# Head norms of an attention stage: one fp32 product with ones, or two one-pass products, and one step later

## The chip, the cores and the metric

The kernel runs on one core of one Trainium2 chip. The metric is the time of one execution on the device in microseconds (us); the median of the runs counts. The engines are named as in the profile: PE (TensorE), ACT (ScalarE), DVE (VectorE), POOL (GpSimd), and SP, which only issues DMAs.

## The reference, cut to what matters

Two layers of a decoder trunk over 512 tokens. Four mixers share one input projection; one of them is a differential attention with 4 heads of 128 value channels. Each head's output is normalised over its own 128 channels:

```python
    a = p[:, :, 0] - lam * p[:, :, 1]
    return jnp.einsum('bhqk,bkhe->bqhe', a.astype(v.dtype), v)
...
o = rmsnorm(o, sub_g) * (1.0 - lambda_init)
```

Then come the output projection, the residual, and a gated feed-forward block.

## The kernel before

Channels lie on the 128 partitions and tokens on the free axis, so a head's output is one tile of 128x512. Every engine runs a list of its own, written out by hand, and semaphores tie the lists together; nothing is scheduled by a planner. The order in the list is the order of work.

Large matmuls are in three one-pass products: the weights as a rounded part `wh` (fp32r, written by ACT in `prep`) and a remainder `wl` (written by POOL in `low`), against a rounded part and a remainder of the activations. One such output tile is a *unit*.

The attention of a layer is a loop over 16 steps, n = 0 to 15, four steps for each head (n // 4 is the head, n % 4 the block of 128 queries). In step n:

- PE does `scores(n + 2)`, `turn(n)` (transposes of the probabilities), at n = 1, 5, 7, 9, 13 and 15 (`BESIDE`) a unit of the output projection, and `attend(n - 1)`. At n = 15 the unit stands ahead of `turn`.
- DVE does `combine(n + 1)` (two softmaxes into one, which `turn(n + 1)` waits for) and `maxima(n + 2)` (which `exps(n + 2)` on ACT waits for). At n % 4 == 0 `head_out` copies the finished head from bank 5 to `ssum`; at n % 4 == 3 `head_emit` scales it.
- ACT does `exps(n + 1)`, the copy of the transposed probabilities (line 1355), and some `prep`s. `scores(n + 2)` takes the banks that `exps(n)` has read.
- POOL does a `low` whenever its weights are there.

The norm of head h is spread over this loop: at n % 4 == 1 ACT squares `ssum` into `pad` (`head_square`, line 1331); at n % 4 == 2 PE, last in its step, multiplies the squares with a matrix of ones in fp32 (`head_sum`, line 963), and ACT takes the logarithm of the mean (`head_log`, line 1336); at n % 4 == 3 ACT makes the reciprocal root of it (`head_rms`, line 1340). For heads 0 to 2 that is n = 5, 6, 7, then 9, 10, 11, then 13, 14, 15; head 3 comes after the loop.

Two other places matter. The norms of q and k in the projection already use a rounded part and a remainder: ACT writes `sq_high` and the square, POOL the difference (line 549), and PE two products with `block_r` (lines 891 and 892). And `block_r`, the fp32r copy of a constant, is made by DVE in layer 0 at s = 8 of the projection, between two copies into `cbf` (lines 2009 and 1653) and ahead of `lambdas` (lines 1656 and 1657). The next step of DVE's list is the scaling of `u` (line 1467) and `m2_turned(2)` (lines 1735 to 1738), which frees bank 4 for `m2_decays(0)` on PE (line 852). POOL meanwhile computes a table (lines 460 to 462) and the remainders of the weights (line 428).

Of the kernel before, what the change touches and what calls it, by code (L numbers as in the profile page):

```python
# [7 lines left out]
F32 = mybir.dt.float32  # L8
F32R = mybir.dt.float32r
BF16 = mybir.dt.bfloat16  # L10
ALU = mybir.AluOpType
ACT = mybir.ActivationFunctionType
# [3 lines left out]
D, T, P = 1024, 512, 128  # L16
KD = D // P
NQ = T // P
HEADS, QK = 4, 64
# [18 lines left out]
BESIDE = [1, 5, 7, 9, 13, STEPS - 1]  # L38
GATES = 3
V_BANK = [0, 1, 6, 7]  # L40
HEAD_BANK = [0, 0, 2, 6]
WHOLE_MEAN = 5
EPS = 1e-6
NIN = 28
FINE, COARSE = 32, 16
# [32 lines left out]
def build(nc, A):  # L78
    with ExitStack() as ctx:
        arena_end = [0]  # L80

        def sb(name, shape, dt=F32, at=None):

            size = int(np.prod(shape[1:])) * (2 if dt == BF16 else 4)
            size = -(-size // 32) * 32
            off = arena_end[0] if at is None else at
            if at is None:
                arena_end[0] += size
            offsets[name] = off
            return nc.alloc_sbuf_tensor_at(name, list(shape), dt, offset=base + off)  # L90

        def sem(name):
            return ctx.enter_context(nc.semaphore(name))
# [57 lines left out]
        for l in range(L):  # L151
# [28 lines left out]
        block_r = sb("block_r", [P, P], F32R)  # L180
        raw2 = sb("raw2", [P, FHALF * P], at=offsets["wglu"])
        raws = [raw[:, 0, :], raw[:, 1, :], raw2[:, :]]
        t_at = [offsets["qk"] + i * 3 * HT * 4 for i in range(2 * KW - 1)] + [offsets["G"] + 4 * T * 4]
        t_his = [sb(f"t_high{k}", [P, 3 * HT], F32R, at=t_at[KW + k]) for k in range(KW)]
        t_los = [sb(f"t_low{k}", [P, 3 * HT], F32R, at=t_at[k]) for k in range(KW)]
# [64 lines left out]
        exp_go, exp_done, probs_ready, probs_turned = [  # L250
            sem(n) for n in ("exp_go", "exp_done", "probs_ready", "probs_turned")]
        token_ready = sem("token_ready")
        head_copied, osq_ready, head_ln, onorm_done = [
            sem(n) for n in ("head_copied", "osq_ready", "head_ln", "onorm_done")]
        g_ready, g_silu, h_ready, h_high, hid_ready = [
            sem(n) for n in ("g_ready", "g_silu", "h_ready", "h_high", "hid_ready")]

# [154 lines left out]
        def _(pool):  # L412
# [112 lines left out]
            for l in range(L):  # L525
                low()
                for s in range(NIN - 1):
                    low()
                    if s == 1:
                        power_terms(l, 0)  # L530
                        nc.gpsimd.memset(kernels[:, :, :, :], 0.0)
                    if 2 <= s <= 4:
                        for n in ((1, 2), (3,), (4, 5))[s - 2]:
                            power_terms(l, n)
                    if s == 5:
                        pool.wait_ge(late_loaded, 32)
                        output_matrix(l)
                    if 6 <= s <= 8:
                        state_terms(l, s - 6)
                    if 9 <= s <= 10:  # L540
                        table(l, 0, s - 9)
                    if 11 <= s <= 12:
                        for n in ((3, 4), (5,))[s - 11]:
                            state_terms(l, n)
                    if 13 <= s <= 14:
                        table(l, 1, s - 13)
                    if 17 <= s <= 24 and s - 17 != WHOLE_MEAN:
                        pool.wait_ge(sqk_ready, 8 * l + s - 16)
                        tt(sq_low[:, :], G[:, 2, :], sq_high[:, :].bitcast(F32), ALU.subtract).then_inc(sqk_low, 1)
                    if s in (15, 21):  # L550
                        s5_imaginary(l, (s - 15) // 6)
                for _ in range(16):
                    low()
                for half in range(2):
                    for _ in range(2 * FHALF):
                        low()
                    if (l, half) in PAIRED:
                        pair_lows(UNIT_AT.index((l, NIN + 16 + 2 * FHALF)) if half == 0 else len(UNITS))
                    else:
                        for _ in range(8):  # L560
                            low()
# [3 lines left out]
        def _(pe):  # L565
# [358 lines left out]
            def scores(n):  # L924
                h, q = n // NQ, n % NQ
                banks = (2, 3, 6, 7)[2 * (n % 2):2 * (n % 2) + 2]
                rows = [slice(QK * c, QK * c + QK) for c in range(2)]
                qs = [qk[r, 2 * h, q * P:(q + 1) * P] for r in rows]
                last = slice(q * P, (q + 1) * P)
                for b in banks:  # L930
                    claim(b, exp_done)
                if q:
                    for c, b in enumerate(banks):
                        mm(bank[b][:, 0:q * P], qs[c], qk[rows[c], 2 * h + 1, 0:q * P], start=True, stop=True)
                for c, b in enumerate(banks):
                    mm(bank[b][:, last], qs[c], qk[rows[c], 2 * h + 1, last], start=True, stop=False)
                for b in banks:
                    mm(bank[b][:, last], cbf[:, 0, :], cbf[:, 1, :], start=False, stop=True).then_inc(dve_bank[b], 1)
# [18 lines left out]
                if q == NQ - 1:  # L957
                    w.then_inc(dve_bank[5], 1)

            def head_sum(b):  # L960
                pe.wait_ge(osq_ready, nth(osq_ready))
                claim(b, head_ln)
                mm(bank[b][:, :], ones, pad[:, 0, 4:4 + T], start=True, stop=True).then_inc(act_bank[b], 1)

            early_hi, early_lo = mh[:, MIXB:MIXED, :], ml[:, MIXB:MIXED, :]
            for l in range(L):
# [73 lines left out]
                for n in range(STEPS):  # L1040
                    if n + 2 < STEPS:
                        scores(n + 2)
                    if n == BESIDE[-1]:
                        unit(1, KEARLY, early_hi, early_lo, resid)
                    turn(n)
                    if n == GATES:
                        s5_glu()
                    if n == BESIDE[0]:
                        pe.wait_ge(mixed_ready, nth(mixed_ready, KEARLY))
                    if n in BESIDE[:-1]:  # L1050
                        unit(BESIDE.index(n) % 2, KEARLY, early_hi, early_lo, resid)
                    if n == 1:
                        pe.wait_ge(v_ready, HEADS * (l + 1))
                    if n:
                        attend(l, n - 1)
                    if n > NQ and n % NQ == 2:
                        head_sum(HEAD_BANK[n // NQ - 1])
                attend(l, STEPS - 1)
                unit(0, KEARLY, early_hi, early_lo, resid)
                head_sum(HEAD_BANK[HEADS - 1])  # L1060
# [15 lines left out]
        def _(act):  # L1076
# [127 lines left out]
            for l in range(L):  # L1204
# [121 lines left out]
                        fn(G[:, 2 * s + c, 0:w], bank[(2, 3, 6, 7)[2 * s + c]][:, 0:w], ACT.Exp,  # L1326
                           bias=soft[:, s, c:c + 1], accum_out=soft[:, s, 2 + c:3 + c]).then_inc(exp_done, 1)

                def head_square():
                    act.wait_ge(head_copied, nth(head_copied))  # L1330
                    fn(pad[:, 0, 4:4 + T], ssum[:, :], ACT.Square).then_inc(osq_ready, 1)


                def head_log(b):
                    act.wait_ge(act_bank[b], nth(act_bank[b]))
                    fn(rbc[:, :], bank[b][:, :], ACT.Ln, scale=1.0 / P, bias=eps).then_inc(head_ln, 1)

                def head_rms(h):
                    act.wait_ge(head_ln, l * HEADS + h + 1)
                    fn(rbc[:, :], rbc[:, :], ACT.Exp, scale=-0.5).then_inc(onorm_done, 1)  # L1340
# [7 lines left out]
                for n in range(STEPS):  # L1348
                    if n + 1 < STEPS:
                        exps(n + 1)  # L1350
                    if n > NQ and n % NQ == 3:
                        head_rms(n // NQ - 1)
                    act.wait_ge(act_bank[4], nth(act_bank[4]))
                    w = (n % NQ + 1) * P
                    fn(G[:, 4 + n % 2, 0:w], bank[4][:, 0:w], ACT.Copy).then_inc(probs_turned, 1)
                    if n == GATES:
                        for i, gate in enumerate((sA, sB)):
                            act.wait_ge(act_bank[i], nth(act_bank[i]))
                            fn(gate[:, :], bank[i][:, :], ACT.Sigmoid, bias=par_of(l, "bglu", i)).then_inc(glu_full, 1)
                        ln_exp_tables()  # L1360
                    if n == GATES + 1:
                        for i, gated in enumerate((sC, sD)):
                            emit(MIXC + i, gated[:, :])
                    if n > NQ and n % NQ == 1:
                        head_square()
                    if n - 1 in BESIDE:
                        prep()
                    if n > NQ and n % NQ == 2:
                        head_log(HEAD_BANK[n // NQ - 1])
                    if n > NQ and n % NQ == 0:  # L1370
                        emit(MIXA + n // NQ - 2, ssum[:, :])
                emit(MIXA + HEADS - 2, ssum[:, :])
# [60 lines left out]
        def _(dve):  # L1433
# [543 lines left out]
            for l in range(L):  # L1977
# [4 lines left out]
                for s in range(2, NIN):  # L1982
# [24 lines left out]
                    if l == 0 and s == 8:  # L2007
                        dve.wait_ge(cst_loaded, 16)
                        copy(cbf[:, 0, :], ident)
                        copy(block_r[:, :], block1).then_inc(block_ready, 1)  # L2010
                        lambdas()
                    if s == 9:
# [241 lines left out]
```

## Time and profile before

| what | us |
|---|---|
| median of 3 runs | 1303.96 (1303.4 to 1304.52) |
| profiled execution | 1304.08 |
| its span, first to last instruction | 1302.3 |
| PE busy | 1280.8 (98%) |
| DVE busy | 995.7 (76%) |
| POOL busy | 637.1 (49%) |
| ACT busy | 534.4 (41%) |

The profile is of one execution. What lies around the span is 1.8 us. The granted clock of PE is 1.00 of full speed over the whole span. Matmuls are pipelined, so a row of PE is longer than the time by which it holds up the next one; the distance of two starts tells that.

### The profile page before, as it was taken

Reading aid. Unit: us, or ns where it says so; the run is one execution under the profiler, and the core shown is the slowest. Engines: PE = TensorE matmul, PEld = TensorE weight load, DVE = VectorE, ACT = ScalarE, POOL = GpSimd, SP = SyncE. Lnnn points to the kernel's source line nnn. Section 1 sums busy time; section 2 is a strip of 40 time slices with the busy share of each in tenths; the row PEclk is TensorE's granted clock in tenths of the full one; section 3 lists DMA queues with packets and bytes.
Section 4 is the critical chain, followed back from the end, with each engine's and each line's share of the span. In section 5 each row is a group of like instructions: output and inputs, shape, how many; then the busy total and the mean of one; then the engine's idle time right before and its main releaser. Section 6 shows DMA issues by size and latency. Waiting matters only on the chain.

```text
span 1302.3 us, 17612 instructions
## 1 busy us (share of the span) xinstructions
PE 1280.8 (98%) x6758; PEld 1071.3 (82%) x6758; DVE 995.7 (76%) x1376; ACT 534.4 (41%) x836; POOL 637.1 (49%) x314
## 2 busy tenths in 40 slices
PE   7999999999999999999999999999999999999999
PEld 4878887788888998888878888867888889988898
DVE  7889894846899868886237798767478997689987
ACT  6332556644233332233334335476442333323332
POOL 2986662144445344444458775612354443444532
PEclk9999999999999999999999999999999999999999
DMA  6232231023333223233223213201333323232323
GB/s 212 79 109 67 81 95 44 25 86 109 99 95 132 90 88 97 95 100 112 84 97 97 82 53 112 79 26 50 98 105 97 97 99 114 95 93 89 125 92 104
DMA packets 40947, 120.59 MB, mean 93 GB/s; under 512 B 6432, under 2 KB 10656, under 8 KB 40864
## 3 DMA queue, kind: packets, MB, share of 16 engines
q1 hardware_dynamic: 40864, 119.46, 29.1%
q8 instruction: 54, 0.88, 0.3%
q14 instruction: 29, 0.24, 0.1%
HBM read 114.20 MB, written 2.10 MB: 89 GB/s over the span
## 4 chain that ended last, share of the span: by engine, by line
PE 75%; DVE 18%; ACT 2%; POOL 2%; issue 2%; DMA 1%; SPq 0%; DVEq 0%; POOLq 0%
PE bank L595 18%; PE bank L608 17%; PE bank L600 16%; PE bank L646 9%; PE bank L907 3%; DVE G L1479 3%; DVE bank L1851 2%; DVE G L1950 1%; DVE G L1478 1%; ACT G L1326 1%; PE bank L955 1%; DMA raw<-in_w_in 1%; PE bank L597 1%; POOL wl L428 1%; DVE G L1467 1%
## 5 line engine op out<-in xcount | busy, mean ns | idle before, releaser
L428 POOL TENSOR_TENSOR wl<-raw,wh 128x1024 fp32r<-128x1024 f32 (+3 forms) x184 | 442.2, 2405 | 520.7 <-ACT wh L1097 427.3
L595 PE MATMUL bank<-xl,wh 128*128 128x512 f32 x1088 | 281.7, 397 | 0.0
L608 PE MATMUL bank<-xh,wl 128*128 128x512 f32 x1088 | 272.4, 392 | 0.0
L600 PE MATMUL bank<-xh,wh 128*128 128x512 f32 x1056 | 261.0, 389 | 0.0
L1097 ACT ACTIVATE wh<-raw 128x1024 fp32r<-128x1024 f32 (+3 forms) x184 | 185.8, 1010 | 144.6 <-PE bank L600 90.9
L595 PEld LDWEIGHTS bank<-xl,wh 128*128 128x128 f32 x1088 | 202.8, 188 | 47.1 <-issue 5.4
L608 PEld LDWEIGHTS bank<-xh,wl 128*128 128x128 f32 x1088 | 203.2, 188 | 43.0 <-issue 1.4
L600 PEld LDWEIGHTS bank<-xh,wh 128*128 128x128 f32 x1056 | 198.2, 188 | 41.6
L445 POOL TENSOR_TENSOR wl<-raw,wh 128x768 fp32r<-128x768 f32 (+1 forms) x36 | 64.9, 1811 | 101.9 <-ACT wh L1101 70.0
L1398 ACT ACTIVATE G<-G 128x512 f32<-128x512 f32 x44 | 27.8, 633 | 181.3 <-DVE G L1479 181.3
L1101 ACT ACTIVATE wh<-raw 128x640 fp32r<-128x640 f32 (+2 forms) x72 | 60.5, 861 | 94.2 <-DVE raw L1917 37.1
L1496 DVE TENSOR_TENSOR x<-x,bank 128x512 f32<-128x512 f32 x40 | 27.4, 684 | 80.2 <-PE bank L608 80.0
L1467 DVE TENSOR_TENSOR G<-bank,rbc 128x512 f32<-128x512 f32 x68 | 46.4, 683 | 34.2 <-PE bank L608 34.2
L1467 DVE TENSOR_TENSOR pad<-bank,rbc 128x512 f32<-128x512 f32 x60 | 41.1, 686 | 38.2 <-PE bank L608 27.3
L595 PE MATMUL bank<-ml,wh 128*128 128x512 f32 x248 | 68.9, 401 | 0.0
L1479 DVE SCALAR_TENSOR_TENSOR G<-pad,par_all,G 128x512 f32<-128x512 f32 x48 | 66.5, 1385 | 1.7
L1474 DVE TENSOR_SCALAR G<-pad,par_all 128x512 f32<-128x512 f32 x48 | 65.5, 1364 | 1.6
L608 PE MATMUL bank<-mh,wl 128*128 128x512 f32 x248 | 63.2, 389 | 0.0
L1899 DVE TENSOR_TENSOR x<-x,bank 128x256 f32<-128x256 f32 (+1 forms) x72 | 41.7, 593 | 24.4 <-PE bank L663 17.0
L600 PE MATMUL bank<-mh,wh 128*128 128x512 f32 x225 | 57.1, 390 | 0.0
L1159 ACT ACTIVATE xh<-x,par_all 128x512 fp32r<-128x512 f32 x32 | 23.1, 721 | 80.0 <-DVE x L1496 77.6
L608 PEld LDWEIGHTS bank<-mh,wl 128*128 128x128 f32 x248 | 46.5, 188 | 9.7
(343 smaller groups left out, 2093.8 us busy)
## 6 DMA issues: line engine op xcount, KB each, us to landing
raw<-in_w_gu SPq DMA_DIRECT2D x88, 512.0 KB, 3.6
raw<-in_w_in SPq DMA_DIRECT2D x52, 512.0 KB, 3.7
raw<-in_w_dn SPq DMA_DIRECT2D x32, 704.0 KB, 4.2
raw<-in_w_ol SPq DMA_DIRECT2D x16, 384.0 KB, 3.0
raw<-in_w_oe SPq DMA_DIRECT2D x16, 256.0 KB, 2.6
x<-in_x SPq DMA_DIRECT2D x8, 256.0 KB, 6.4
raw<-in_w_first SPq DMA_DIRECT2D x4, 512.0 KB, 4.7
out_x<-x SPq DMA_DIRECT2D x8, 256.0 KB, 4.6
```

The lines of the kernel that those rows point to most:

```text
L428: tt(wl[:, p, 0:cols], raws[RAW[g][0]][:, 0:cols], wh[:, p, 0:cols].bitcast(F32), ALU.subtract).then_inc(wl_full, 1)
L445: tt(wl[:, p, cols], raws[PAIR_RAW[load][0]][:, cols], wh[:, p, cols].bitcast(F32), ALU.subtract).then_inc(pair_low, 1)
L595: mm(bank[b][:, :], wh[:, p, k * P:(k + 1) * P], lo[:, k, :], start=(k == 0), stop=False)
L600: w = mm(bank[b][:, :], wh[:, p, k * P:(k + 1) * P], hi[:, k, :], start=False, stop=False)
L608: w = mm(bank[b][:, :], wl[:, p, k * P:(k + 1) * P], hi[:, k, :], start=False, stop=(k == K - 1))
L646: i = mm(out, w[:, at[0], at[1] + k * P:at[1] + (k + 1) * P], b, start=start and k == 0, stop=stop and k == KW - 1, skip_group_check=True)
L1097: fn(wh[:, p, 0:cols], raws[r][:, 0:cols], ACT.Copy).then_inc(wh_full, 1)
L1101: fn(wh[:, p, to], raws[PAIR_RAW[2 * j + p][0]][:, of], ACT.Copy).then_inc(pair_high, 1)
L1467: tt(out, bank[b][:, :].rearrange(order, **sizes), rbc[:, :].rearrange(order, **sizes), MUL).then_inc(unit_out, 1)
L1474: after(ts(out, pad[:, p, 4:4 + T], weights[n - 1], None, MUL))
L1479: return stt(out, pad[:, p, 5 - n:5 - n + T], weights[0], out, MUL, ADD)
L1899: tt(out, out, b, ADD).then_inc(pair_read, 1)
```

## The change

For heads 0 to 2, `head_square` writes the square twice: rounded to fp32r into `xh[:, 0, :]`, and whole into `pad`. POOL writes the difference into `xl[:, 0, :]`, in its list ahead of the `low`s 3, 5 and 6 of the output projection. PE multiplies both parts with `ones_r`, an fp32r copy of the ones, in two one-pass products into one bank. `head_sum` moves from the end of step n % 4 == 2 to step n % 4 == 3, behind `scores(n + 2)` and ahead of the unit of n = 15 and of `turn(n)`. `head_log` moves from the end of ACT's step n % 4 == 2 into n % 4 == 3, behind `exps(n + 1)` and right ahead of `head_rms`. The banks are 1, 0, 0 instead of 0, 0, 2. Head 3 stays as it was. `ones_r` is made by DVE right ahead of `block_r`.

```diff
-HEAD_BANK = [0, 0, 2, 6]
+HEAD_BANK = [1, 0, 0, 6]
+HEAD_LOW = [3, 5, 6]
...
+        ones_r = sb("ones_r", [P, P], F32R)
...
-                for _ in range(16):
+                for n in range(16):
+                    if n in HEAD_LOW:
+                        pool.wait_ge(osq_ready, l * HEADS + HEAD_LOW.index(n) + 1)
+                        tt(xl[:, 0, :], pad[:, 0, 4:4 + T], xh[:, 0, :].bitcast(F32), ALU.subtract).then_inc(osq_low, 1)
                     low()
...
-            def head_sum(b):
+            def head_sum(b, parts=False):
+                if parts:
+                    nth(osq_ready)
+                    pe.wait_ge(osq_low, nth(osq_low))
+                    claim(b, head_ln)
+                    mm(bank[b][:, :], ones_r[:, :], xh[:, 0, :], start=True, stop=False)
+                    mm(bank[b][:, :], ones_r[:, :], xl[:, 0, :], start=False, stop=True).then_inc(act_bank[b], 1)
+                    return
...
                     if n + 2 < STEPS:
                         scores(n + 2)
+                    if n > NQ and n % NQ == 3:
+                        head_sum(HEAD_BANK[n // NQ - 1], True)
                     if n == BESIDE[-1]:
                         unit(1, KEARLY, early_hi, early_lo, resid)
                     turn(n)
...
-                    if n > NQ and n % NQ == 2:
-                        head_sum(HEAD_BANK[n // NQ - 1])
...
-                def head_square():
+                def head_square(parts=False):
                     act.wait_ge(head_copied, nth(head_copied))
+                    if parts:
+                        fn(xh[:, 0, :], ssum[:, :], ACT.Square)
                     fn(pad[:, 0, 4:4 + T], ssum[:, :], ACT.Square).then_inc(osq_ready, 1)
...
                     if n > NQ and n % NQ == 3:
+                        head_log(HEAD_BANK[n // NQ - 1])
                         head_rms(n // NQ - 1)
...
                     if n > NQ and n % NQ == 1:
-                        head_square()
+                        head_square(True)
                     if n - 1 in BESIDE:
                         prep()
-                    if n > NQ and n % NQ == 2:
-                        head_log(HEAD_BANK[n // NQ - 1])
...
                         copy(cbf[:, 0, :], ident)
+                        copy(ones_r[:, :], ones)
                         copy(block_r[:, :], block1).then_inc(block_ready, 1)
```

## Rows read from the trace of the kernel before

**Rows 1.** The page: the span, and the chain that ended last, shares by engine.
```profile
span 1302.3 us, 17612 instructions
...
PE 75%; DVE 18%; ACT 2%; POOL 2%; issue 2%; DMA 1%; SPq 0%; DVEq 0%; POOLq 0%
```

**Rows 2.** Waits, 76 to 90 us: us in total, times, longest.
```profile
PE bank L852 <- DVE xbt L1738: 1.1, 1, 1.1
```

**Rows 3.** The chain in order of time, layer 0: start us, us, what.
```profile
248.51 0.86 PE bank L963 x2
```

**Rows 4.** Timeline of PE, q/k norms: start us, us, engine, line.
```profile
146.10 0.39 PE L891 MATMUL bank<-sqk_high,block_r 128*128 128x512 f32 x1
146.33 0.39 PE L892 MATMUL bank<-sqk_low,block_r 128*128 128x512 f32 x1
```

**Rows 5.** Timeline of PE, attention of layer 0, [idle before <-releaser].
```profile
236.47 0.66 PE L944 MATMUL bank<-cst,G 128*128 128x128 f32 x4 [0.54 <-DVE G L1834]
...
249.30 0.49 PE L934 MATMUL bank<-qk 64*128 64x128 f32 x4
...
250.13 0.66 PE L944 MATMUL bank<-cst,G 128*128 128x128 f32 x4
...
253.62 0.92 PE L934 MATMUL bank<-qk 64*128 64x384 f32 x4
...
259.03 1.02 PE L963 MATMUL bank<-pad,cst 128*128 128x512 f32 x2
```

**Rows 6.** Timeline of ACT, attention of layer 0.
```profile
247.06 0.69 ACT L1326 ACTIVATE G<-bank,soft 128x512 f32<-128x512 f32 x1 [1.21 <-DVE soft L1825]
...
251.01 0.62 ACT L1340 ACTIVATE rbc<-rbc 128x512 f32<-128x512 f32 x1
251.53 0.59 ACT L1355 ACTIVATE G<-bank 128x512 f32<-128x512 f32 x1
252.46 0.47 ACT L1326 ACTIVATE G<-bank,soft 128x256 f32<-128x256 f32 x1 [0.33 <-DVE soft L1825]
...
256.93 0.63 ACT L1331 ACTIVATE pad<-ssum 128x512 f32<-128x512 f32 x1 [0.28 <-DVE ssum L1841]
...
261.00 0.69 ACT L1336 ACTIVATE rbc<-bank,eps 128x512 f32<-128x512 f32 x1
261.73 0.63 ACT L1340 ACTIVATE rbc<-rbc 128x512 f32<-128x512 f32 x1
```

**Rows 7.** Timeline of DVE, attention of layer 0.
```profile
243.12 1.35 DVE L1492 TENSOR_TENSOR ml<-ssum,mh 128x512 fp32r<-128x512 f32 x1 [0.50 <-ACT mh L1187]
...
248.74 0.55 DVE L1833 TENSOR_SCALAR G<-G,soft,mlam_all 128x512 f32<-128x512 f32 x1
249.33 0.75 DVE L1834 SCALAR_TENSOR_TENSOR G<-G,soft 128x512 f32<-128x512 f32 x1
```

**Rows 8.** Timeline of POOL: a remainder of the q/k norms, a weights' remainder.
```profile
149.23 1.30 POOL L549 TENSOR_TENSOR sqk_low<-G,sqk_high 128x512 fp32r<-128x512 f32 x1 [0.41 <-ACT G L1226]
...
242.64 1.27 POOL L428 TENSOR_TENSOR wl<-raw,wh 128x512 fp32r<-128x512 f32 x1 [5.09 <-ACT wh L1097]
```

**Rows 9.** Timeline of DVE, layer 0, s = 8 of the projection.
```profile
79.87 0.21 DVE L2010 CAST block_r<-cst 128x128 fp32r<-128x128 f32 x1
80.01 1.29 DVE L1653 CAST cbf<-pre 128x128 bf16<-128x128 f32 x1
81.22 0.28 DVE L1656 TENSOR_TENSOR lprod<-pre 128x128 f32<-128x128 f32 x1
...
81.85 2.05 DVE L1656 TENSOR_TENSOR lprod<-pre 128x128 f32<-128x128 f32 x1
```

**Rows 10.** Timeline of POOL in the same stretch.
```profile
79.94 1.27 POOL L462 TENSOR_TENSOR s5f<-s5f,s5h 128x512 f32<-128x512 f32 x1
81.29 2.46 POOL L428 TENSOR_TENSOR wl<-raw,wh 128x1024 fp32r<-128x1024 f32 x1
83.71 1.38 POOL L460 TENSOR_TENSOR s5g<-rot 128x512 f32<-128x512 f32 x1
```

More of the change, by code:

```diff
@@ L252, in build @@
         token_ready = sem("token_ready")
-        head_copied, osq_ready, head_ln, onorm_done = [
-            sem(n) for n in ("head_copied", "osq_ready", "head_ln", "onorm_done")]
+        head_copied, osq_ready, osq_low, head_ln, onorm_done = [
+            sem(n) for n in ("head_copied", "osq_ready", "osq_low", "head_ln", "onorm_done")]
         g_ready, g_silu, h_ready, h_high, hid_ready = [
```

## The prediction

> **What bounds the kernel now.** I read the page first: PE is busy for 98% of the span of 1302.3 us, and the chain that ended last runs over PE for 75% and over DVE for 18% [rows 1]. So a shorter product may pay, but only where PE doesn't wait for someone else straight after it. Then I read the waits and the timelines of all engines around each of the six products that change, and around the one new copy. The reader is to look there for who was late at the next hand-over, not at how busy an engine is.
>
> **The product itself.** The fp32 product with ones holds the chain for 0.86 us [rows 3]. Two one-pass products of the same shape already stand in the trace, 0.23 us apart [rows 4]; two of them are 0.46 us. Six products make 6 x 0.40 = 2.4 us, the most that the change can give. Where does it go?
>
> **Heads 0 and 1: the 0.40 us are lost in front of `turn`.** At step 7, `turn(7)` on PE waited 0.54 us for DVE's `combine(7)` [rows 5]. That combine hangs on `exps(7)` and DVE's own queue, neither of which needs `head_sum(0)`. Nothing that ends before that hand-over brings it forward. The moved product of 0.46 us fits into the wait of 0.54. Gain 0, loss 0. At step 11, `turn(11)` began at 250.13 [rows 5], 0.05 us after `combine(11)` ended (249.33 + 0.75 = 250.08 [rows 7]); I take 0.05 as the cost of a hand-over. Without `head_sum(1)` `scores(13)` (249.30 [rows 5]) may start up to 0.86 us sooner, but the new 0.46 us come behind it and `turn(11)` still waits for 250.08. Gain between 0 and 0.05; I take 0. On layer 1 the timeline repeats these starts 641.3 us later with the same gaps.
>
> **The second square on ACT** costs 0.52 us, the distance of two ACT instructions of 512 columns (251.01 to 251.53 [rows 6]). The next work, `exps` of the following step, had ACT idle for 1.21 us before it, waiting for DVE [rows 6]; that hides it. Were that idle time gone, it would cost 0.52 per head.
>
> **The logarithm moves behind `exps(n + 1)`.** There it takes 0.73 us (261.00 to 261.73 [rows 6]) ahead of the reciprocal root and of line 1355's copy. After head 1, the root was at 251.01 and the copy at 251.53 [rows 6]; they go to 251.74 and 252.26. The copy then ends at 252.85, and `exps(13)`, which started at 252.46 after 0.33 us of idle time, can't start before about 252.76 (the next instruction overlaps the tail by 0.10, as 0.62 against 0.52 shows). So `exps(13)` is 0.30 late, bounds 0 and 0.73. Who waits for it? `scores(15)` on PE, which started at 253.62 [rows 5], and `combine(13)` on DVE, from which DVE works without a gap to `combine(14)`, that is to `turn(14)`. I put the full 0.30 us on the path of each layer. After head 0 the same delay meets a unit on PE and a DVE that is busy with `residual`; I take 0 there. What is queued behind the logarithm on ACT is only this copy and the `exps`; the `prep` that stood ahead of it now runs no later.
>
> **Head 2: PE waits for POOL.** At n = 15 there are no `scores` left, so the product stands where it stood, directly behind `attend(13)`, at 259.03 [rows 5] + 0.30 = 259.33. The new remainder is not there yet: the square began at 256.93 [rows 6]; with 0.30 delay, a second square (0.52 later, 0.63 long, as the first) ends at 258.38; POOL starts at 258.43 and takes 1.30, like the same difference for q and k [rows 8], to 259.73; PE starts at 259.78 and is done at 260.24. Before it was 259.03 + 0.86 = 259.89. So head 2 saves nothing: +0.35 us against before, the 0.30 included. Two layers: **+0.70**. Bounds: 0 (ACT's overlap is larger) and 2 x 0.73 + 2 x 0.5 (nothing hidden) = 2.5.
>
> **POOL's list.** Each difference comes before a `low` whose weights ACT has not yet prepared (`low` 4 waited 5.09 us for them [rows 8]), so the queue behind the new wait is not held up, nor SP's loads, which wait for `low`. But POOL and DVE disturb each other: while POOL ran 242.64 to 243.91 [rows 8], DVE's subtraction of two SBUF operands took 1.35 us from 243.12 on [rows 7], some 0.67 more than the usual one. For head 1 the first square ended at 247.06 - 1.21 = 245.85 [rows 6], the second one ends at 246.37, POOL works from 246.42 to about 247.7, and DVE's next instruction on SBUF alone is at 248.74 [rows 7]. In between it works on PSUM. Cost 0, with 1.0 us in hand; bound 1.27 each.
>
> **The copy `ones_r` is the large term.** It looks like 0.14 us of DVE (79.87 to 80.01 [rows 9]), once. But `m2_decays(0)` on PE, line 852, waited 1.1 us for DVE at the end of just this sequence [rows 2], and no wait of PE stands between it and the attention, so what DVE loses here PE loses. And DVE doesn't lose 0.14. In the rows DVE's small instructions and POOL's take turns: `block_r` at 79.87 got in before POOL's 79.94; the next, at 80.01, took 1.29 us and ended at 81.30, when POOL's was over (79.94 + 1.27 = 81.21) [rows 9, 10]. The product at 81.22 got in before POOL's 81.29; the one at 81.85 took 2.05 us, to 83.90, over POOL's end at 83.75 [rows 9, 10]. With one more copy, `ones_r` takes the place of `block_r`, and `block_r` that of the cast at 80.01, to 81.30. The cast takes the place at 81.22, and the first product comes 0.14 later, at 81.36, behind POOL's 81.29. It ends at 83.90, where the second one used to end. The second follows 0.35 later (81.50 to 81.85 before), at 84.25, and POOL's next instruction holds until 83.71 + 1.38 = 85.09 [rows 10]; it ends at 85.24. DVE is 1.34 us late, and so is line 852. I take **+1.34**; bounds 0.14 (0 even, if the turn at 81.85 swallows it) and 2.64 (one more POOL instruction of 1.30 lost).
>
> The Trainium skill, page "SBUF — State Buffer", section "SBUF: two separate sides", says that the port pair which VectorE and GpSimd share is an exclusive lock held for a whole instruction, taken by whichever starts first, and that VectorE wants it with two SBUF inputs or in a two-port mode. The starts and ends above agree with it. By it the copy costs a turn; by the copy's own row, 0.14. It speaks against this change.
>
> **The sum:** 1304.08 (profiled execution; span plus 1.8 around it) + 0.70 + 1.34 = 1306.1. The median of the runs is 0.12 lower than that execution: **1306.0**, or 0.16% slower. A measurement of this kernel can tell about 0.2%, here 2.6 us: slower begins at 1306.6, faster ends at 1301.4.
>
> **Rivals.** *The copy is hidden.* If DVE keeps its turn at 81.36 (it lies only 0.07 behind POOL), the first product ends by 81.7, the second still ends at 83.90, and only the attention's 0.70 is left: 1304.7. For it: the margin is thin. Against: the cast at 80.01 lost with the same 0.07. *A second turn lost:* POOL's next instruction gets in before the product that waits at 85.09. +1.30, 1307.3, slower. Against it: at 83.71 the waiting DVE went first, and POOL's took 1.38. *Faster:* PE is the bound at each of the six places and no wait takes up the 0.40: 1304.0 - 2.4 = 1301.6, about at the edge of what can be told. Against it stand the 0.54 at step 7 and the 0.05 at step 11; it decides only if the `combine`s end 0.4 sooner. *POOL's difference blocks `combine`:* it would have to start after 248.74 - 1.27 = 247.47, which is 1.0 later than worked out; 1.27 for head 1 of each layer: 1308.5.
>
> **How the numbers follow.** Forecast 0.52, its own range 1305.2 to 1306.8; copy hidden 0.25; second turn lost 0.12; `combine` blocked 0.05; all six gained 0.03; and 0.03 for a gain of a part. From the forecast some 0.08 and from the two slow rivals 0.17 lie above 1306.6: slower 0.25. Faster 0.02. Same 0.73. The range for 8 in 10 takes in the hidden copy and most of the second turn: 1303.9 to 1307.4.
>
> **What would show it.** In the profile after: two products 0.23 apart between `scores(9)` and `turn(7)`, and `turn(7)` still waiting for DVE; ACT without idle time before `exps(13)`; PE waiting some 0.45 us for POOL's difference at n = 15; line 852 waiting 2.4 us instead of 1.1, and DVE's first line 1656 taking over 2 us. If line 852 still waits 1.1 to 1.3, the largest term is wrong. If `turn(7)` and `turn(11)` come sooner relative to the layer's first `scores`, the argument on heads 0 and 1 is wrong.

## The result and the profile after

The changed kernel takes 1307.58 us (median of 9 runs, 1306.32 to 1308.1), the kernel before 1303.84 us (9 runs): a ratio of 1.0028, 95% interval [1.002, 1.0036]. That is 3.7 us more; 2.0 us were forecast, with a range up to 1307.4, and a time more than 0.2% longer had been given a chance of 0.25. The profiled execution took 1307.58 us over a span of 1305.8 us, 3.5 us more than before.

The waits of PE in the changed kernel (line, whom it waited for: us in total, times, longest; line 719 of before is 724 now, 852 is 857, 934 is 939, 944 is 949, `head_sum` is 970 and 971):

```profile
PE bank L724 <- ACT wh L1109: 9.0, 1, 9.0
PE bank L939 <- ACT G L1338: 5.8, 10, 1.2
PE bank L857 <- DVE xbt L1751: 2.5, 1, 2.5
PE bank L970 <- DVE x L1509: 1.8, 2, 0.9
PE bank L651 <- DVE x L1912: 1.7, 3, 0.6
PE bank L949 <- DVE G L1847: 1.1, 2, 0.5
PE bank L949 <- ACT G L1370: 0.9, 2, 0.5
```

Line 857 waited 1.1 us before [rows 2] and waits 2.5 now, as forecast. But the products with ones wait for `DVE x`, that is for the residual, 0.9 us in each layer, and no step of the prediction knew of that. The two waits of 0.5 us for ACT's line 1370 are new too. That line 939 waits 5.8 us, where line 934 waited 4.1, is no loss: ahead of `scores(9)` stands a wait of 1.2 us in each layer, in the place that head 0's product has left.

To see where the time comes in, take the starts of the transposes: those of step 0 and step 15 of an attention enclose everything that the change moved. The kernel before, then the changed one, layer 0, from the timeline of PE:

```profile
211.83 0.33 PE L944 MATMUL bank<-cst,G 128*128 128x128 f32 x1
...
262.64 0.60 PE L944 MATMUL bank<-cst,G 128*128 128x128 f32 x4
```

```profile
213.08 0.33 PE L949 MATMUL bank<-cst,G 128*128 128x128 f32 x1
...
264.95 0.60 PE L949 MATMUL bank<-cst,G 128*128 128x128 f32 x4
```

Step 0 starts 1.25 us later, all of it from line 857. From there to step 15 it is 50.81 us before and 51.87 after: +1.06. Layer 1 gives 50.82 and 51.85, +1.03. The rest, between the layers and behind them, is 0.16. Together 3.50, the difference of the spans. So the term for the copy was right (1.34 forecast, 1.25 found), and the attention costs 1.05 per layer instead of 0.35.

**The copy.** DVE and POOL in s = 8 of the projection in the changed kernel, to set beside [rows 9, 10]:

```profile
79.87 0.21 DVE L2023 CAST ones_r<-cst 128x128 fp32r<-128x128 f32 x1
80.01 1.29 DVE L2024 CAST block_r<-cst 128x128 fp32r<-128x128 f32 x1
81.22 0.21 DVE L1666 CAST cbf<-pre 128x128 bf16<-128x128 f32 x1
81.36 2.48 DVE L1669 TENSOR_TENSOR lprod<-pre 128x128 f32<-128x128 f32 x1
...
84.20 0.96 DVE L1669 TENSOR_TENSOR lprod<-pre 128x128 f32<-128x128 f32 x1
```

```profile
79.95 1.28 POOL L464 TENSOR_TENSOR s5f<-s5f,s5h 128x512 f32<-128x512 f32 x1
81.30 2.39 POOL L430 TENSOR_TENSOR wl<-raw,wh 128x1024 fp32r<-128x1024 f32 x1
83.65 1.36 POOL L462 TENSOR_TENSOR s5g<-rot 128x512 f32<-128x512 f32 x1
```

`ones_r` has the place that `block_r` had, `block_r` the one of the long cast. The cast falls into the gap at 81.22, and the first product of the lambdas at 81.36 comes 0.06 behind POOL's 81.30: it takes 2.48 us. The second one then waits over POOL's 83.65 as well, until 85.16. An instruction of 0.14 us has cost 1.25.

**The attention.** PE in the changed kernel, layer 0, around the three products:

```profile
237.02 0.48 PE L970 MATMUL bank<-xh,ones_r 128*128 128x512 f32 x1
237.33 0.39 PE L971 MATMUL bank<-xl,ones_r 128*128 128x512 f32 x1
237.75 0.65 PE L949 MATMUL bank<-cst,G 128*128 128x128 f32 x4
...
251.43 0.66 PE L949 MATMUL bank<-cst,G 128*128 128x128 f32 x4
...
254.30 0.30 PE L949 MATMUL bank<-cst,G 128*128 128x128 f32 x1 [0.47 <-ACT G L1370]
...
259.81 0.52 PE L949 MATMUL bank<-cst,G 128*128 128x128 f32 x3
...
261.67 0.47 PE L970 MATMUL bank<-xh,ones_r 128*128 128x512 f32 x1 [0.89 <-DVE x L1509]
261.98 0.39 PE L971 MATMUL bank<-xl,ones_r 128*128 128x512 f32 x1
```

Heads 0 and 1 went as worked out: `turn(7)` and `turn(11)` start 1.28 and 1.30 us later than in [rows 5], which is the shift of step 0 with 0.03 and 0.05 more; the products fit into the waits and neither cost nor gave anything. Head 2 is where it went wrong. `turn(14)` starts at 259.81 (before 258.19), +1.62, so 0.37 came from the late `exps(13)` (0.30 forecast). Then the first product at 261.67 had 0.89 us of idle time before it, and what it waited for is bank 0. ACT, DVE and POOL at that point:

```profile
248.36 0.69 ACT L1338 ACTIVATE G<-bank,soft 128x512 f32<-128x512 f32 x1 [0.69 <-DVE soft L1838]
...
253.57 0.58 ACT L1370 ACTIVATE G<-bank 128x512 f32<-128x512 f32 x1
254.05 0.47 ACT L1338 ACTIVATE G<-bank,soft 128x256 f32<-128x256 f32 x1
...
259.06 0.62 ACT L1345 ACTIVATE pad<-ssum 128x512 f32<-128x512 f32 x1
```

```profile
260.84 0.68 DVE L1509 TENSOR_TENSOR x<-x,bank 128x512 f32<-128x512 f32 x1
```

```profile
259.75 1.27 POOL L557 TENSOR_TENSOR xl<-pad,xh 128x512 fp32r<-128x512 f32 x1 [7.24 <-ACT pad L1345]
```

POOL's difference was there at 259.75 + 1.27 = 261.02, but DVE's `residual`, which reads bank 0 after the unit of step 13, ran from 260.84 to 261.52. It stands in DVE's list behind `maxima(15)`, which DVE worked on until 260.93. The two products then held the unit behind them up by 0.53 us (261.67 to 262.20), not by 0.46. The copy at 253.57 is the one that `turn(12)` waited for (line 1370), and the `exps` at 248.36 still had 0.69 us of idle time ahead of it with a second square before it.

### The profile page after: what moved, and what is told of

Read it like the earlier page. It is cut to its first block, busy times and chain, and to the rows that moved or that the text cites. A ratio compares the mean times of both kernels' runs of the same rounds, so it can differ in the third digit from the quotient of the medians.

```text
span 1305.8 us, 17625 instructions
## 1 busy us (share of the span) xinstructions
PE 1279.3 (98%) x6758; PEld 1071.6 (82%) x6758; DVE 996.6 (76%) x1377; ACT 538.0 (41%) x842; POOL 648.4 (50%) x320
## 4 chain that ended last, share of the span: by engine, by line
PE 77%; DVE 15%; ACT 3%; POOL 2%; DMA 1%; issue 1%; SPq 0%; DVEq 0%; POOLq 0%
PE bank L600 19%; PE bank L613 19%; PE bank L605 18%; PE bank L651 10%; PE bank L912 3%; DVE bank L1864 2%; DVE G L1492 2%; ACT G L1338 1%; DMA raw<-in_w_in 1%; PE bank L602 1%; DVE soft L1838 1%; POOL wl L430 1%; DVE G L1491 1%; DVE G L1847 1%; DVE G L1846 1%
## 5 line engine op out<-in xcount | busy, mean ns | idle before, releaser
L1487 DVE TENSOR_SCALAR G<-pad,par_all 128x512 f32<-128x512 f32 x48 | 65.8, 1370 | 1.6
```

Of the source, the lines that this page charges most:

```text
L1487: after(ts(out, pad[:, p, 4:4 + T], weights[n - 1], None, MUL))
```

## The experiments

The measure for most of them is the time from the transposes of step 0 to those of step 15 in a layer: 50.81 us before (50.82 in layer 1), 51.87 and 51.85 in the changed kernel. The profiled execution gives this to a few hundredths, while whole runs scatter by about 1 us: in the traces with the wait at line 852 or 857, PE comes to it between 83.4 and 86.1 us, of which the wait at the very start (8.2 to 9.8 us) is a part. So the division of the loss rests on the profiled executions and their waits. The kernel before was run 21 to 29 times beside each group of experiments, medians 1303.4 to 1303.8.

**e1: the copy elsewhere.**

```diff
-                        copy(ones_r[:, :], ones)
                         copy(block_r[:, :], block1).then_inc(block_ready, 1)
...
+                if l == 0:
+                    copy(ones_r[:, :], ones)
                 maxima(0)
```

> The changed kernel, with the copy into ones_r taken out of s = 8 of the projection and put right ahead of the attention of layer 0. Theory (the copy costs DVE a turn against POOL, and line 857 on PE waits for that): 1.2 to 1.3 us less than the changed kernel, about 1306.3, and line 857 waits 1.1 us again instead of 2.45. Rival (the copy costs only its own 0.14 us, the later wait has another cause): 1307.4, line 857 waits over 2 us.

Measured: 1305.89 us, ratio 1.0016 [1.0007, 1.0025], by the two ratios 1.6 us less than the changed kernel. Its waits:

```profile
PE bank L970 <- DVE x L1509: 1.8, 2, 0.9
...
PE bank L857 <- DVE xbt L1751: 1.1, 1, 1.1
```

Line 857 is back at 1.1 us, the attention is as in the changed kernel (51.85 and 51.86). The rival falls.

**e2: bank 2 for head 2.**

```diff
-HEAD_BANK = [1, 0, 0, 6]
+HEAD_BANK = [1, 0, 2, 6]
```

> The changed kernel, with head 2's product in bank 2, as before the change, instead of bank 0. Theory (at n = 15 PE waits for DVE's residual, which reads bank 0 until 0.6 us after POOL's remainder is there): the wait before the first product is 0.3 to 0.4 us instead of 0.89 and names POOL; 0.5 to 0.6 us less in each layer, about 1306.5. Rival (PE waits for POOL's remainder there, the bank is free in time): no change, 1307.6.

Measured: 1306.83 us, ratio 1.0023 [1.0013, 1.0032]; 51.29 us in both layers, 0.57 less than the changed kernel. The product now waits for POOL, in the timeline of PE and of POOL:

```profile
261.84 0.50 PE L970 MATMUL bank<-xh,ones_r 128*128 128x512 f32 x1 [0.30 <-POOL xl L557]
262.18 0.39 PE L971 MATMUL bank<-xl,ones_r 128*128 128x512 f32 x1
```

```profile
260.52 1.27 POOL L557 TENSOR_TENSOR xl<-pad,xh 128x512 fp32r<-128x512 f32 x1 [7.24 <-ACT pad L1345]
```

POOL ends at 261.79 and the product starts at 261.84. In the changed kernel the bank came 0.5 us after this. That is the step that was missing.

The same trace shows a second price of the copy, which the changed kernel's own trace doesn't have. PE behind the wait of line 857, in the changed kernel and in e2:

```profile
87.42 1.16 PE L857 MATMUL bank<-cst,s 128*128 128x128 f32 x8 [2.45 <-DVE xbt L1751]
88.42 1.06 PE L849 MATMUL bank<-xbc 128*128 128x128 f32 x8
```

```profile
86.61 1.20 PE L857 MATMUL bank<-cst,s 128*128 128x128 f32 x8 [2.31 <-DVE xbt L1751]
87.60 1.91 PE L849 MATMUL bank<-xbc 128*128 128x128 f32 x8
```

The same eight products of line 849 take 1.91 us instead of 1.06, and the eight of line 613 behind them 2.94 instead of 2.09. In e2 PE stood idle for 2.31 us, worked for about 1 us with the granted clock still at 1.00, and then the clock was 0.50 of full speed from 88 to 91 us (the lower of its two levels, 1.2 GHz) and 1.00 again from there on. In the changed kernel it was 1.00 throughout. From line 857 to the transposes of step 0 it is 127.26 us in e2 and 125.66 in the changed kernel: 1.6 us. e4's trace has the same (127.27, idle time 2.35 us). Runs whose mean clock is below 1.00, as e2's and e4's profiled ones are, number 16 of 34 in the four kernels that have the copy at s = 8 (1 of 9 of the changed one, 5 of 9 of e2, 6 of 11 of e3, 4 of 5 of e4), and 1 of 112 in the other experiments. Why some executions fall into this and others with as long a wait don't was not tried.

**e3: the copy alone, in the kernel before.**

```diff
                         copy(cbf[:, 0, :], ident)
+                        copy(ones_r[:, :], ones)
                         copy(block_r[:, :], block1).then_inc(block_ready, 1)
```

> The kernel before, with only the copy into ones_r added ahead of block_r; nothing reads it. Theory (a lost turn): 1.2 to 1.3 us more than before, about 1305.1, the first product of line 1656 takes over 2 us. Rival (0.14 us, or hidden): 1303.8 to 1304.0.

Measured: 1305.93 us, ratio 1.002 [1.0011, 1.0029]. The wait, at line 853 here:

```profile
PE bank L853 <- DVE xbt L1739: 2.4, 1, 2.4
```

2.4 us instead of 1.1, and the attention untouched (50.83, 50.84). A copy that nothing reads costs 1.3 us by the wait. The whole runs give 2.5 (1.4 to 3.8), more than that. In this trace, whose clock was 1.00, the other 1.05 us lie ahead of the wait, which is within the scatter given above. But 6 of its 11 runs have a clock below 1.00; at 1.6 us each (an estimate from e2's trace) that is 0.9 us of the mean. So a copy of 0.14 us costs 1.2 to 1.3 us in each of the four traces that have it, and in 16 of 34 runs probably another 1.6.

**e4: ACT's copy first.**

```diff
-                    if n > NQ and n % NQ == 3:
-                        head_log(HEAD_BANK[n // NQ - 1])
-                        head_rms(n // NQ - 1)
                     act.wait_ge(act_bank[4], nth(act_bank[4]))
...
                     fn(G[:, 4 + n % 2, 0:w], bank[4][:, 0:w], ACT.Copy).then_inc(probs_turned, 1)
+                    if n > NQ and n % NQ == 3:
+                        head_log(HEAD_BANK[n // NQ - 1])
+                        head_rms(n // NQ - 1)
```

> The changed kernel, with ACT's copy of the transposed probabilities ahead of the logarithm and the root in steps 7, 11 and 15. turn(12) then no longer waits 0.47 us for that copy. Theory (what reaches turn(14) is the late exps(13), by way of DVE, and that stays): no change, within 0.2 us of 1307.6. Rival (the wait of turn(12) reaches the end): 0.4 to 0.5 us less in each layer, about 1306.7.

Measured: 1310.65 us, ratio 1.0055 [1.0041, 1.0068]. Both were wrong about the time, and the theory was right about its own point. `turn(12)` doesn't wait any more, and yet from step 0 to step 14 it takes 46.69 us, as in the changed kernel (46.73). `scores(15)` waits 0.37 us for `exps(13)` instead. But:

```profile
PE bank L975 <- ACT pad L1345: 2.8, 2, 1.4
```

At n = 15 the order matters in the other direction. The logarithm of head 2 now stands behind a copy that has to wait for the late `turn(15)`; so `head_emit`, DVE's copy of head 3 and its square come later, and PE waits 1.4 us per layer for that square. The expectation had looked only at head 1. Part of this run's time is also the lower clock of e2, in four of its five runs.

**e5: the split without the move.** `ones_r` made as in e1, the two products at the old place, banks 0, 0, 2, the logarithm at its old place:

```diff
-                    if n > NQ and n % NQ == 3:
-                        head_sum(HEAD_BANK[n // NQ - 1], True)
...
                         attend(l, n - 1)
+                    if n > NQ and n % NQ == 2:
+                        head_sum(HEAD_BANK[n // NQ - 1], True)
```

> The two one-pass products in the old place (end of step n % 4 == 2), the old banks and the old place of the logarithm; ones_r made right ahead of the attention. Only the split is left of the change. Theory (the 0.40 us that a product saves are taken by the wait for DVE's combine at heads 0 and 1, and by the wait for POOL's remainder at head 2): from the first to the last transposes of a layer's attention 50.8 to 51.0 us, as before (50.81), and 0 to 0.2 us per layer more than the kernel before: the same time as before within 0.4 us. Rival (the saving reaches the end where nothing is moved): 0.4 per head, 49.6 us per layer, 2.4 us less than before.

Measured: 1303.99 us, ratio 1.0006 [0.9997, 1.0015]; 51.03 and 50.97 us. Three shorter products give nothing, even where nothing is moved; it is 0.2 us per layer more than before. PE waits for POOL at heads 0 and 2 (1.2 us in 4 waits), and the other places are covered by the waits for `combine`.

**e6: the move without the split.** The kernel before with one fp32 product ahead of `turn(n)`, banks 1, 0, 0, the logarithm ahead of the root:

```diff
+                    if n > NQ and n % NQ == 3:
+                        head_sum(HEAD_BANK[n // NQ - 1])
                     if n == BESIDE[-1]:
...
-                    if n > NQ and n % NQ == 2:
-                        head_sum(HEAD_BANK[n // NQ - 1])
...
+                        head_log(HEAD_BANK[n // NQ - 1])
                         head_rms(n // NQ - 1)
```

> The kernel before with only the move: one fp32 product a step later, banks 1, 0, 0, the logarithm ahead of the root; no second square, no remainder, no ones_r. Theory (the move is what costs, by the bank that waits for DVE's residual at head 2, and here also by the longer product between the scores and the transposes at heads 0 and 1): from the first to the last transposes 52.8 us against 51.87 of the changed kernel and 50.81 before; about 4 us more than before. Rival (the remainder and the second square are what costs): no more than the changed kernel's attention without them, 50.8 to 51.3 us per layer.

Measured: 1306.97 us, ratio 1.0027 [1.0017, 1.0038]; 52.40 us in both layers, less than the 52.8 expected, since the longer product costs only 0.20 us in front of `turn(7)` (3.85 us from step 6 instead of 3.65). The move alone loses 1.6 us per layer. The same wait for the residual is there without POOL's remainder and without a second square:

```profile
259.57 1.10 PE L963 MATMUL bank<-pad,cst 128*128 128x512 f32 x2 [0.89 <-DVE x L1495]
```

**e7: the constants of layer 0 later.** The kernel before with this block of DVE behind `m2_turned(3)`:

```diff
-                    if l == 0 and s == 8:
-                        dve.wait_ge(cst_loaded, 16)
-                        copy(cbf[:, 0, :], ident)
-                        copy(block_r[:, :], block1).then_inc(block_ready, 1)
-                        lambdas()
```

> The kernel before, with the small copies and the lambda products of DVE in s = 8 of layer 0 put behind m2_turned(3) of s = 9; nothing else. Theory (PE's line 852 waits 1.1 us only because these instructions lose two turns against POOL ahead of m2_turned(2)): that wait is gone, 1.0 to 1.1 us less than before. Rival (DVE's scaling of u or POOL is what it waits for in the end): the wait stays above 0.5 us and the time is that of before.

Measured: 1302.94 us, ratio 0.9997 [0.9988, 1.0006]. The wait at line 852 is gone, but 0.8 us of it are found a few instructions on, at the next product that needs DVE:

```profile
PE bank L834 <- DVE hst L1752: 0.8, 1, 0.8
```

So the theory was right about line 852 and wrong about the gain, and the rival had the time right: it can't be told from that of before.

**e8: a run that was not what its expectation says.**

> The changed kernel with both mends: ones_r copied right ahead of the attention, head 2's product in bank 2. Theory (a lost turn of 1.3 us once, and 0.57 us per layer for the bank, are independent): 51.29 us from the first to the last transposes of a layer, line 857 waits 1.1 us; 1.0 to 1.1 us more than the kernel before, 2.4 less than the changed one. Rival (they hide one another): more than 1.6 us above the kernel before.

The kernel that ran had e4's order on ACT besides the two mends. Measured: 1307.81 us, ratio 1.0031 [1.0019, 1.0042], with e4's wait of 2.8 us in all for the square of head 3. It is 3.5 us more than e14, which differs from it by e4's order alone. So this order costs as much without the other two losses; of the mends themselves the run tells nothing. e14 below is the kernel that was meant.

**e9: head 2 alone, the remainder inside the next unit.** The kernel before, the constants as in e7 (with `ones_r`). Head 2's rounded part is multiplied at the old place in bank 2; the remainder's product comes inside the unit of n = 15:

```diff
+                    if middle is not None and part == 0:
+                        middle()
                     if ready is None:
...
+            def head_rest(b):
+                pe.wait_ge(osq_low, nth(osq_low))
+                mm(bank[b][:, :], ones_r[:, :], xl[:, 0, :], start=False, stop=True).then_inc(act_bank[b], 1)
```

> The kernel before with the constants as in the run above (with ones_r), and two one-pass products for head 2 alone: the rounded part's product in the old place and bank, the remainder's product inside the unit that follows, after its first pass of four products. Heads 0, 1 and 3 as before. Theory (head 2 is the one of heads 0 to 2 whose product PE does not wait after, and POOL's remainder is 0.5 us late only for the first place): 0.40 us less per layer from the first to the last transposes (50.4 instead of 50.81), together 1.8 to 1.9 us less than before. Rival (something behind head 2 takes it up, the logarithm or the root for the last head): only the 1.1 us of the constants.

Measured: 1303.16 us, ratio 0.9996 [0.9987, 1.0005]; 50.42 and 50.43 us. So one product does give its 0.39 us, at the only one of the three places where PE does not wait afterwards. The 1.1 us of the constants did not come: the wait at DVE's `hst` was 1.5 us here. The whole run can't be told from the kernel before, where 1.8 to 1.9 us less were expected.

**e13: no wait for POOL at head 2.** As e14 below, but head 2's second product takes `xh` again; the remainder is left out of it. PE takes POOL's semaphore only behind the unit that follows.

```diff
+                        mm(bank[b][:, :], ones_r[:, :], xh[:, 0, :], start=True, stop=False)
+                        mm(bank[b][:, :], ones_r[:, :], xh[:, 0, :], start=False, stop=True).then_inc(act_bank[b], 1)
```

> As the run before, but head 2's second product takes the rounded part once more instead of the remainder, so it leaves the remainder out and does not wait for POOL; the work of each engine stays the same. Theory (what is left of head 2's loss is 0.3 us of waiting for POOL): 51.0 us from the first to the last transposes instead of 51.29; the remaining 0.2 above the 50.81 of before is exps(13) behind the logarithm, less what the shorter product gives. Rival (all that is left comes from the late exps): 51.29, unchanged.

Measured: 1303.79 us, ratio 1.0002 [0.9993, 1.0011]; 50.71 and 50.69 us. The gain over e2 is 0.58, twice what I expected. The row of the wait says 0.30. But rows of PE are longer than what they hold up: with the wait gone the first product starts 0.72 us behind `turn(14)` (259.44 against 258.72), before the row of `attend(13)` ends, and in e2 it started 1.27 us behind it. Here the idle time in a row was only about half of what the wait cost.

**e14: both mends.**

> The changed kernel with the two mends alone: ones_r copied right ahead of the attention, head 2's product in bank 2; ACT's order as in the changed kernel. Theory (the lost turn and the bank are independent): 51.29 us from the first to the last transposes of each layer, line 857 waits 1.1 us, 0.9 to 1.1 us more than the kernel before. Rival (they hide one another): over 51.6 us or over 2 us of wait at line 857.

Measured: 1304.33 us, ratio 1.0004 [0.9996, 1.0013]; 51.26 and 51.28 us, line 857 waits 1.2 us. In the trace the two losses are independent and add up. With them gone whole runs can't be told from the kernel before; by the trace 0.45 us per layer is still lost.

**e15: the logarithm of heads 0 and 1 short.** As e14; those two take it of one column of 512 and leave out the rest.

```diff
+                    if h < 2:
+                        fn(rbc[:, 0:1], bank[b][:, 0:1], ACT.Ln, scale=1.0 / P, bias=eps).then_inc(head_ln, 1)
+                        return
```

> As the run before, but the logarithm of heads 0 and 1 is taken of one column of 512 only, so it leaves out the rest. Theory (the moved logarithm makes exps(13) some 0.3 to 0.4 us late and that reaches the transposes of step 14): from the transposes of step 0 to those of step 14 46.4 us as before the change (46.36) instead of 46.7; the first to the last 50.9 to 51.0. Rival (the second square or the longer way over POOL makes it late): 46.7, unchanged.

Measured: 1304.16 us, ratio 1.0003 [0.9994, 1.0012]; 46.36 and 46.39 us from step 0 to step 14, before the change 46.36, with the whole logarithm 46.72. So up to step 14 the logarithm ahead of `exps(13)` costs 0.36 us (0.32 in layer 1), and the second square none of it. Up to step 15 the run takes 50.97 and 51.02 us, 0.29 and 0.26 less than e14: a little of it is taken up at head 2.

**e11: two copies to where DVE is idle.** The kernel before, with two of the copies at the end of s = 16:

```diff
                         dve.wait_ge(cst_loaded, 16)
-                        copy(cbf[:, 0, :], ident)
-                        copy(block_r[:, :], block1).then_inc(block_ready, 1)
                         lambdas()
...
+                        if l == 0:
+                            copy(cbf[:, 0, :], ident)
+                            copy(block_r[:, :], block1).then_inc(block_ready, 1)
```

> The kernel before, with only the copies into cbf (the identity) and block_r moved from s = 8 to s = 16 of layer 0, where DVE is idle for 4.5 us; the mask and the lambda products stay. Theory (without them the two lambda products fall into the gaps between POOL's instructions, and m2_turned(2) and m2_state come 1.1 us or more sooner): no wait of PE at lines 852 and 834, 1.0 to 1.1 us less than before. Rival (as when the constants were put behind m2_turned(3), the wait only moves): 0.3 us less or nothing.

Measured: 1302.6 us, ratio 0.9994 [0.9985, 1.0003]. PE has no wait at lines 852 or 834 in its trace; the median of 11 runs is 0.8 us lower, which the interval doesn't separate from nothing.

**e12: the two ideas together.** e11's place for the copies, and e9's way for heads 2 and 3.

> The kernel before with those copies (and ones_r) at s = 16, and two one-pass products for heads 2 and 3, the remainder's product inside the unit that follows; heads 0 and 1 stay one fp32 product. Theory (PE does not wait after heads 2 and 3, so each gives 0.40 us per layer): 50.42 us from the first to the last transposes, another 0.4 per layer behind them, together with the copies 2.6 to 2.7 us less than before. Rival (head 3's later logarithm holds up the last product of the output projection's first late unit): a wait of PE behind the attention, and no more than 1.9 us less than before.

Measured: 1301.32 us, ratio 0.9984 [0.9975, 0.9993]: 2.1 us less than the kernel before and by the two ratios 5.7 less than the changed one, the only version here that is faster beyond its interval. From step 0 to step 15 it is 50.48 us in layer 0. All that is left of the waits of PE:

```profile
PE bank L727 <- ACT wh L1114: 8.2, 1, 8.2
PE bank L942 <- ACT G L1343: 4.1, 10, 0.5
PE bank L952 <- DVE G L1853: 2.2, 4, 0.5
PE bank L654 <- DVE x L1918: 1.7, 3, 0.6
```

No wait of PE's products for the square or the logarithm of head 3 has come up, and the 2.6 to 2.7 us expected lie within the interval. But head 3 gives nothing. From step 15 of layer 0 to step 0 of layer 1 it is 590.49 us, 590.49 in e11 and 590.50 before; from step 15 of layer 1 to the end of the span 398.4 us in all three. The two products hold up the unit around them by 0.34 us each (264.05 to 264.39 and 265.42 to 265.76), and their weight loads wait 0.30 us for ACT's square and 0.38 for POOL's remainder. So the gain within a layer is head 2's alone, 0.33 and 0.36 us, and the rest of what e12 gives lies ahead of the first attention, where the 1.1 us of line 852 are gone.

## Why the prediction was wrong, point by point

- **The copy `ones_r` costs a turn against POOL: right.** 1.34 forecast, 1.25 in the trace. e1 takes it away, e3 puts it alone into the kernel before. The instructions went as the prediction laid them out one by one. The exclusive lock of the port pair that the Trainium skill describes (page "SBUF — State Buffer", section "SBUF: two separate sides") is borne out again: started 0.06 us behind POOL's instruction of 2.39 us, DVE's product took 2.48 us where it had taken 0.28 [rows 9]. What the prediction has no term for is the lower clock behind the longer wait, 1.6 us in e2's and e4's traces; of the 9 runs of the changed kernel 1 has a clock below 1.00, so it is no part of the 3.7 us.
- **Heads 0 and 1 give nothing: right.** `turn(7)` starts 0.05 us behind the end of `combine(7)` (236.95 + 0.75 = 237.70), 0.06 behind it before; `turn(11)` likewise. The wait itself no longer shows in PE's row, since the products fill it. e5 shows the same for the old place.
- **The second square is hidden: right.** The idle time before the next `exps` fell from 1.21 to 0.69 us, and e15 leaves no share for it.
- **The logarithm makes `exps(13)` 0.30 late: right, 0.36** (e15). The prediction named two ways to `turn(14)`, `scores(15)` on PE and `combine(13)` on DVE. It is DVE's: DVE works from 255.10 to 259.73 without a wait, and in e4 step 13 comes 0.23 us sooner after step 0 (43.30 instead of 43.53) and step 14 doesn't. `turn(12)` waited as well, 0.47 us, for the copy behind the logarithm, and no step of the prediction has that. It doesn't add: e4 removes it and step 14 comes no earlier.
- **Head 2's product starts when POOL's remainder is there: the step that failed.** "Before it was 259.03 + 0.86 = 259.89. So head 2 saves nothing: +0.35 us against before". It put what the bank costs at nothing, without a reason: the change moves this product from bank 2 to bank 0, and the prediction has no term and no bound for when bank 0 comes free. DVE takes the `residual` that reads it up only behind `maxima(15)`, so bank 0 is free 0.5 us after POOL is done. e2 puts it at 0.57 us per layer, 1.14 in all, and e6 shows the same wait without POOL. The wait for POOL was also too small, 0.45 against 0.58 (e13): without it the product would start 0.72 us behind `turn(14)`, where the fp32 product had started 0.84 behind it (258.19 to 259.03).
- **The account of one layer:** +0.36 for the late `exps` (up to step 14; e15 confirms it), -0.46 for the shorter product (e13: from step 14 to step 15 3.99 us instead of 4.45; 0.12 of it is the earlier start), +0.58 for POOL (e2 less e13), +0.57 for the bank (changed kernel less e2). Sum 1.05; measured 1.06 and 1.03. The terms are differences along one chain of kernels, so that they add up is no proof of their own; the prices of POOL and of the bank hold in this order, the bank's on top of POOL's. The prediction had +0.30 - 0.40 + 0.45 + 0.

So the sign was right and the size was not: 2.0 instead of 3.7 us by the medians, 2.0 instead of 3.5 in the traces. Of the 1.5 us that the traces miss the bank is 1.1. None of the rivals on record was this one.

## What to carry to other kernels

Go through every semaphore that a moved instruction waits for, the bank it writes above all, and look up where the one who frees it stands in the list of its own engine now, not where its data was last touched. A shorter product pays only where PE doesn't wait right behind it: of six places that was so at two (head 2 of each layer), and there the longer way to its operands took the gain. And before an instruction is added to DVE's list, see whether it lies in a stretch where DVE and POOL take turns at SBUF: its price there can be one of POOL's instructions, not its own duration. A longer wait of PE can also cost what comes behind it: look at the granted clock after the wait, and in all runs, not in one trace.

## What the runs showed of the hardware

- The first of the two one-pass products holds the second one up by 0.31 us, and not by 0.23 as in [rows 4], where larger one-pass products precede them: 237.02 to 237.33, 261.67 to 261.98. It is 0.34 us where the weights were loaded only as the product started (e2: 261.84 to 262.18; e12, head 3). Why wasn't tried.
- Between two POOL instructions that follow each other without a wait, a waiting instruction of DVE gets its turn: the product from 81.36 ended at 83.84, 0.15 us behind the end of POOL's first (81.30 + 2.39 = 83.69) and before POOL's next had ended. With it goes the next one of DVE's, if it starts before POOL's does: `ones_r` at 79.87 (POOL 79.95) and the cast at 81.22 (POOL 81.30) took 0.21 us, while `block_r` at 80.01 and the product at 81.36, 0.06 us behind POOL's starts, waited.
- About 1 us behind 2.3 us of idle time the granted clock of PE fell to 0.50 for some 3.4 us in two traces (e2, e4), and stayed at 1.00 behind 2.4 to 2.5 us of idle time in two others (changed kernel, e3). It cost 1.6 us.
